# Moving the second expert's slot comparisons and index products behind the first expert's gather

## What is computed

```python
def ec_moe(h, p):
    B, L, D = h.shape
    T = B * L
    xt = h.reshape(T, D)
    aff = jax.nn.softmax((xt @ p["w_router"]).astype(F32), axis=-1)
    cap = (EC_CAPACITY_FACTOR * T) // N_EXPERTS
    vals, idx = lax.top_k(aff.T, cap)
    xs = xt[idx]
    hid = jax.nn.silu(jnp.einsum("ecd,edf->ecf", xs, p["w_e_gate"])) * jnp.einsum("ecd,edf->ecf", xs, p["w_e_up"])
    ye = jnp.einsum("ecf,efd->ecd", hid, p["w_e_down"]) * vals[..., None].astype(h.dtype)
    y = jnp.zeros((T, D), h.dtype).at[idx.reshape(-1)].add(ye.reshape(-1, D))
    return y.reshape(B, L, D)
```

## Time and profile before

| | |
|---|---|
| median of 3 runs | 3411.35 (3409.85 to 3414.39) |
| the profiled execution | 3411.03, its span 3408.8 |
| PE busy | 3189.8 (94%) |
| DVE busy | 1602.2 (47%) |
| ACT busy | 1270.6 (37%) |
| POOL busy | 377.2 (11%) |
| DMA, mean over the span | 166 GB/s |
| mean granted clock of PE | 0.963 |

### The profile page before, as it was taken

How to read it: one execution, slowest core, us unless ns; L and a number is a source line. 1 busy time by engine, 2 the same in 40 slices (tenths; PEclk the granted TensorE clock), 3 DMA queues, 4 the chain that set the end, 5 groups by cost and what they waited for, 6 DMA issues and landing times. The chain is left out here.

```text
span 3408.8 us, 51857 instructions
## 1 busy us (share of the span) xinstructions
PE 3189.8 (94%) x19543; PEld 2717.6 (80%) x19543; DVE 1602.2 (47%) x2955; ACT 1270.6 (37%) x1953; POOL 377.2 (11%) x358
## 2 busy tenths in 40 slices
PE   7899998999899699999989975999999999999996
PEld 2488887898745699989987765888898988898985
DVE  5433222433256442333225567555555555565556
ACT  4743342422243031222124542444444443444435
POOL 1111111000034100000000001111111111111122
PEclk9999999999899799999999986999999999999998
DMA  8733333321299751432115443555555555555557
GB/s 332 246 127 104 105 117 105 120 76 61 76 362 350 249 175 58 130 100 98 57 70 188 163 170 122 181 194 184 179 186 177 175 175 175 186 197 195 193 206 272
DMA packets 282678, 565.68 MB, mean 166 GB/s; under 512 B 23464, under 2 KB 162472, under 8 KB 278329
## 3 DMA queue, kind: packets, MB, share of 16 engines
q1 hardware_dynamic: 258063, 503.84, 42.6%
q0 software_dynamic: 15456, 54.88, 5.5%
q10 hardware_dynamic: 8976, 4.46, 0.4%
HBM read 434.45 MB, written 128.64 MB: 165 GB/s over the span
## 5 line engine op out<-in xcount | busy, mean ns | idle before, releaser
L71 PE MATMUL experts_bank<-experts_xT_high,experts_w_high_gu 128*128 128x272 f32 x2048 | 597.9, 292 | 6.3 <-DVE experts_w_low_gu L3050 5.7
L73 PE MATMUL experts_bank<-experts_xT_high,experts_w_low_gu 128*128 128x272 f32 x2048 | 591.9, 289 | 0.0
L72 PE MATMUL experts_bank<-experts_xT_low,experts_w_high_gu 128*128 128x272 f32 x2048 | 589.5, 288 | 0.0
L71 PEld LDWEIGHTS experts_bank<-experts_xT_high,experts_w_high_gu 128*128 128x128 f32 x2048 | 385.9, 188 | 19.6 <-issue 12.3
L72 PEld LDWEIGHTS experts_bank<-experts_xT_low,experts_w_high_gu 128*128 128x128 f32 x2048 | 387.0, 189 | 3.9
L73 PEld LDWEIGHTS experts_bank<-experts_xT_high,experts_w_low_gu 128*128 128x128 f32 x2048 | 386.0, 188 | 0.0
L3050 DVE TENSOR_TENSOR experts_w_low_gu<-experts_w_raw_gu,experts_w_high_gu 128x1024 fp32r<-128x1024 f32 x256 | 302.2, 1215 | 12.7 <-ACT experts_w_high_gu L2846 12.7
L2846 ACT ACTIVATE experts_w_high_gu<-experts_w_raw_gu 128x1024 fp32r<-128x1024 f32 x256 | 257.3, 1047 | 14.5 <-DMA experts_w_raw_gu<-in_w_stream 14.4
L71 PE MATMUL merge_pg<-merge_hT_high,merge_w_gates_high 128*128 128x436 f32 (+1 forms) x640 | 231.9, 362 | 10.0 <-DVE merge_hT_low L2111 10.0
L72 PE MATMUL merge_pg<-merge_hT_low,merge_w_gates_high 128*128 128x436 f32 (+1 forms) x640 | 231.5, 362 | 0.0
L73 PE MATMUL merge_pg<-merge_hT_high,merge_w_gates_low 128*128 128x436 f32 (+1 forms) x640 | 230.9, 361 | 0.0
(11 more groups left out here) (395 smaller groups left out, 6588.3 us busy)
## 6 DMA issues: line engine op xcount, KB each, us to landing
experts_w_raw_gu<-in_w_stream SPq DMA_DIRECT2D x256, 512.0 KB, 5.7
experts_w_raw_d<-in_w_stream SPq DMA_DIRECT2D x128, 512.0 KB, 7.1
filters_wm<-in_w_mod SPq DMA_DIRECT2D x12, 2048.0 KB, 11.7
merge_hT<-scratch_hT SPq DMA_DIRECT2D x32, 436.0 KB, 6.7
scratch_h<-out_row SPq DMA_DIRECT2D x17, 520.0 KB, 2.9
x_early<-in_xs SPq DMA_DIRECT2D x17, 512.0 KB, 5.3
scratch_hT<-tokens_hT SPq DMA_DIRECT2D x17, 512.0 KB, 4.4
scratch_qkT<-tokens_qkT SPq DMA_DIRECT2D x17, 512.0 KB, 2.8
```

The costliest lines, as they stand in the source:

```text
L71: pe.matmul(out, lhs[0], rhs[0], start=start, stop=False)
L72: pe.matmul(out, lhs[0], rhs[1], start=False, stop=False)
L73: return pe.matmul(out, lhs[1], rhs[0], start=False, stop=stop)
```

## The change

The comparisons of expert 1 leave the stretch between the numbers of expert 0 and the splits of column 0; eight of them are made in column 0 of expert 0, eight and the context one in column 1. The index products of expert 1 leave PE's list ahead of the body and stand behind the first down product of expert 0, in column 1. The numbers of expert 1 are made at the end of column 2. The comparisons of expert 2, which in expert 0's body were three to a column from column 0, are made four to a column in columns 3 to 6, with the context one in column 7. From expert 1 on everything is as before.

```diff
@@ PE
                     mm.then_inc(*P0.inc(f"g{n}"))
-                index(1)
 
                 def body(e, h, k, one, two):
                     for f in range(KT):
...
                         if f:
                             down(e, f - 1)
+                        if e == 0 and f == 1:
+                            index(1)
@@ DVE
                 numbers(0, 0, 0)
-                v.wait_ge(PI.sem, PI.at(0, "ids"))
-                for n in range(NLAT):
-                    passed(1, n)
-                passed_context(1)
                 for at in range(LEAD):
                     split(0, at)
...
                 keep(0, 0)
-                numbers(1, 1, 0)
 
                 def body(e, h, k, one, two):
                     for f in range(KT):
...
-                        if two and f < 6:
+                        if e == 0 and f < 2:
+                            if f == 0:
+                                v.wait_ge(PI.sem, PI.at(0, "ids"))
+                            for n in range(8 * f, 8 * f + 8):
+                                passed(1, n)
+                            if f == 1:
+                                passed_context(1)
+                        if e == 0 and 3 <= f:
+                            if f == 3:
+                                v.wait_ge(PI.sem, PI.at(1, "ids"))
+                            for n in range(4 * f - 12, min(4 * f - 8, NLAT)):
+                                passed(2, n)
+                            if f == KT - 1:
+                                passed_context(2)
+                        if e and two and f < 6:
                             if f == 0:
                                 v.wait_ge(PI.sem, PI.at(e + 1, "ids"))
                             for n in range(3 * f, min(3 * f + 3, NLAT)):
...
+                        if e == 0 and f == 2:
+                            numbers(1, 1, 0)
```

## The result

3417.77 us in the median of 20 runs (3414.49 to 3422.65) against 3410.43 for the kernel before (20 runs, 3407.84 to 3415.22): a ratio of 1.0021, 95% interval 1.0015 to 1.0027. The change made the kernel 7.3 us slower, 0.2%; 3415.2 had been forecast, 3.9 over the median known then. The profiled execution of after took 3416.70 us (span 3414.5), 5.7 over that of before.

What follows compares the result with a forecast made beforehand. PE's unbroken row from expert 0's first column was taken to bound the kernel: its start and additions move the end. Terms 2.0 + 0.2 + 1.1 + 0.8 = 4.1 us gave 3415.2 us, range 3410.5 to 3418.8.

Steps and rivals of the forecast that it cites:

- Before the change the moved work is free; PE's row decides: Ahead of expert 0's first column: moved work lay under the gather; its start and additions to PE's row move the end.
- The carry is caught by the splits, +2.0: POOL's small addition ahead of gather 0 takes 2.25 us beside two splits, not 0.19; first transfer +2.0 us, bounds 0 to +2.0.
- The collision, +0.2, bounds -0.8 to +0.7: DMA engines at gather 0: splits release weight loads 4.8 us earlier, in front of the gather; +0.2 us on its second transfer.
- Index products in PE's row, +1.1: PE in expert 0, column 1: 33 index products have no cover and add 1.1 us, bounds 1.0 and 1.2.
- Comparisons in DVE's columns, 0: DVE in expert 0's columns: `full` about 0.6 us late in column 1, but nothing near waits for it; 0 us.
- Gather 1, +0.8, 0 to 2.8: Expert 0, column 4: gather 1 has 8.3 us from first issue, needs about 9.1; PE stalls 0.8 us.
- POOL not caught: Rival at gather 0: the carry is not held by the splits; about 3412.5 us, no change; chance 0.20.
- Comparisons starving the gather: Rival at gather 0: DVE's comparisons had slowed its second transfer, so 1.8 us come back; 3413.1 or 3410.3 us; chance 0.06.
- Gather 1 far too late: Rival at PE, column 4 of expert 0: 3.5 us or more of stall, 3418.5 to 3420 us; chance 0.12.

Runs made afterwards that it cites:

- e4: Changed kernel, with SP's load of the first piece of column 2 waiting until gather 0's second transfer has landed; 3413.83 us, ratio 1.0010 to the kernel before.
- e10: The changed kernel itself once more, for a second profile and more runs; 3417.26 us, ratio 1.0018 to the kernel before.
- e1: Changed kernel, with DVE's two splits of column 0 waiting for POOL's carry ahead of gather 0; 3416.96 us, ratio 1.0017 to the kernel before.
- e2: Changed kernel, with DVE's two splits of column 0 waiting until gather 0's first transfer has landed; 3413.91 us, ratio 1.0008 to the kernel before.
- e11: Same kernel as e2 (changed kernel, splits waiting for gather 0's first landing), run again; 3411.69 us, ratio 1.0002 to the kernel before.
- e3: Kernel before, with only DVE's two splits of column 0 put ahead of the comparisons of expert 1; 3415.70 us, ratio 1.0014 to the kernel before.
- e6: Kernel before, with its two splits of column 0 waiting until gather 0's first transfer has landed; 3411.93 us, ratio 0.9999 to the kernel before.
- e7: Kernel before, first split of column 0 behind DVE's first input subtraction, second behind the last; 3412.43 us, ratio 0.9999 to the kernel before.

## Why the prediction was right in its range and short in its size

- *Before the change the moved work is free; PE's row decides.* Right: in the changed kernel's list of PE's waits up to 3318 stand only waits ahead of the first column, and the starts at column 4 show 0.2 more; the later first column and the added products both arrived at the end.
- *The carry is caught by the splits, +2.0.* The mechanism was right, 2.19 us for the forecast 2.25. The first issue moved by only 1.5, since the 0.64 us between carry and issue shrank to 0.18. In e4, which keeps the held carry and takes the loads away, it cost 1.3.
- *The collision, +0.2, bounds -0.8 to +0.7.* This is the step that failed. It measured +2.8 (changed kernel against e4), outside its bounds. In the forecast's own terms the second transfer was to land 6.6 to 8.1 us behind the first issue (7.4 before); it landed 10.0 behind it. The working took 373 GB/s for the loads and let the gather follow them at full rate. From 2086.5 to 2091 the engines moved 250 GB/s, almost all for the loads, though they were busy for 84% of the time, and 0.46 MB of the loads were still to come when the gather began. The row taken as upper bound, expert 2's gather, also stood behind three loads (issued from 2195.24 to 2197.02, its own first issue at 2200.87). But there the engines moved them faster; the stretch 2203 to 2204 of the kernel before, loads alone:

```profile
DMA packets 112, 0.42 MB, mean 418 GB/s; under 512 B 10, under 2 KB 10, under 8 KB 112
```

Why the same kind of load moved at 250 GB/s here and at 418 there no run shows. The forecast's other thought, that the first eight transposes must be done before the second eight, cost 0.1 us here and 0.5 in e10.
- *Index products in PE's row, +1.1.* Right: 2118.49 to 2119.47 is 0.98, and 0.10 more at the hand-over (0.23 from L71 to L72 where 0.12 is usual).
- *Comparisons in DVE's columns, 0.* Right: behind its first column PE never waited for DVE in expert 0, even in column 1, where they reach to the start of `full`.
- *Gather 1, +0.8, 0 to 2.8.* Right in kind, too large: 0.2 on average over seven profiles, and that by two misses of opposite sign. The carry was put at 3.3 us and took 2.24, and the first issue followed it in 0.14 us instead of 0.6 (2128.02 + 2.24 to 2130.40): 9.8 us were left instead of 8.3. Against that the transfers took 9.6 to 10.3 us from first issue to last landing (e1, e2, e4, e10, e11), where 9.1 had been taken. On the carry the weighing of rule and row went the wrong way: the rule of the Trainium skill (SBUF — State Buffer, "Who interferes with whom"), by which one-input DVE work outside the two-port modes holds nothing, would have given 2.2. But e3 speaks against the rule in turn, there comparisons held a gather issue for 4.1 us, and so do thirteen carries of 3.03. The comparisons also read one number of `pos` per partition from SBUF; whether that counts as a second input no run tests.
- *Rivals.* POOL not caught: fell, 2.19 us in every profile with that order. Comparisons starving the gather: fell, by e6 and e7. Gather 1 far too late: fell, 0.6 us at most where 3.5 were needed. The time came near the edge to the slower side all the same, by the collision.

With the collision at 2.8 and the others as measured the sum is 1.3 + 2.8 + 1.1 + 0.2 = 5.4. The two series of the changed kernel say 7.3 (5.1 to 9.2 by its interval) and 6.1 (3.1 to 9.2). The remaining one to two microseconds have no place in a profile. The low stretch behind the first column alone varies by 3.2 us between profiles, worth 1.5; that it makes up the rest is not shown. That the time still fell inside the stated range is in part luck: the room up to 3418.8 had been put there for 2.8 us of stall at gather 1 and a later clock. The stall didn't come, and the collision, outside its own bounds, used the room.

## What to carry to other kernels

When work is taken out from between a producer and a slow transfer, ask what moves up into the gap: here two ready weight splits did, and through them the prefetch that they release. Two DVE passes over two SBUF inputs each, just behind the instruction that woke GpSimd, held a one-column GpSimd addition for their whole 2.2 us and the transfers behind it for 1.5; an indirect DMA issue beside them lost only 0.5 (e1). A prefetch that reached the DMA engines first cost an urgent gather 2.8 us. Cover that does nothing visible may be keeping the order; a wait on the urgent transfer, put ahead of the cheap work, keeps it openly.

## What had not been expected of the hardware

- Queues do not share evenly where one is ahead. While three loads of 512 KB were under way, a gather issued 1.2 us behind them had moved 0.02 MB by 4.4 us behind its own first issue, the loads 1.10 MB; and in e1 a first issue 0.8 us ahead of the loads did not save the second transfer, issued 1.2 us behind the first of them: 9.1 us instead of 6.0.
- The same comparisons hold a GpSimd issue or do not: 1.17 us where the issue came 1.0 us after they had begun behind the two numbers, 4.11 us where they followed two-input splits without a gap. And the carry behind two splits was held through three comparisons in thirteen rows of the kernel before (3.03 us), but not through four in the changed kernel (2.24 us). What decides is open.
- After a carry that was held, POOL's next issue followed in 0.18 us instead of 0.64, so a delay of 2.0 us at the carry arrived as 1.5 at the transfer.
